# Two loads swapped and the first pieces of a step put in another order, in a one-core encoder trunk

## The reference, cut to what matters

```python
D_MODEL = 1024; SEQ = 256; N_MEM = 256
D_FF = ((8 * D_MODEL // 3 + 127) // 128) * 128      # 2816

def rms_norm(x, g):
    xf = x.astype(jnp.float32)
    y = xf * lax.rsqrt(jnp.mean(xf * xf, axis=-1, keepdims=True) + EPS)
    return (y * g.astype(jnp.float32)).astype(x.dtype)

def swiglu_half_step(h, norm_g, w_gate_up, w_down):
    hn = rms_norm(h, norm_g)
    gate, up = jnp.split(hn @ w_gate_up, 2, axis=-1)
    return h + 0.5 * ((jax.nn.silu(gate) * up) @ w_down)

# in every layer i, h = x at first:
h = swiglu_half_step(h, ffn1_norm[i], ffn1_w_gate_up[i], ffn1_w_down[i])
z = rms_norm(h, mix_norm[i]) @ w_in[i]
# memory attention: kv = rms_norm(mem, mem_norm_g) @ w_mem_kv, then softmax(q k) v
h = h + jnp.concatenate([y_mix, y_mem], axis=-1) @ w_out[i]
h = swiglu_half_step(h, ffn2_norm[i], ffn2_w_gate_up[i], ffn2_w_down[i])
```

## Time and profile before

| | before |
|---|---|
| median of three runs | 964.34 us |
| profiled execution, its own time | 966.0 us |
| profiled execution, span from first to last instruction | 964.2 us |
| TensorE busy | 946.4 us, 98% |
| VectorE busy | 557.1 us, 58% |
| ScalarE busy | 462.8 us, 48% |
| mean granted clock of TensorE | 0.991 |
| moved by DMA | 167.06 MB, mean 173 GB/s |

### The profile page before, as it was taken

How to read it: one execution, slowest core, us unless ns; L and a number is a source line. 1 busy time by engine, 2 the same in 40 slices (tenths; PEclk the granted TensorE clock), 3 DMA queues, 4 the chain that set the end, 5 groups by cost and what they waited for, 6 DMA issues and landing times.

```text
span 964.2 us, 13364 instructions
## 1 busy us (share of the span) xinstructions
PE 946.4 (98%) x4482; PEld 778.9 (81%) x4482; DVE 557.1 (58%) x680; ACT 462.8 (48%) x644; POOL 40.9 (4%) x71
## 2 busy tenths in 40 slices
PE   8899999999999999999999999999989999999998
PEld 5788888887888888888878888888867888888887
DVE  5555464584566655454777455556665666455553
ACT  5554453564446444444555354454564365354451
POOL 1000100100000000000100000000120000000000
PEclk9999999999999999999999999999997999999999
DMA  9766756555037746565276656565520256656551
GB/s 300 227 197 208 235 178 216 163 158 176 30 110 232 217 153 207 172 195 197 88 222 215 217 156 205 162 209 183 174 88 1 88 179 217 215 158 207 160 172 44
DMA packets 136704, 167.06 MB, mean 173 GB/s; under 512 B 10600, under 2 KB 101456, under 8 KB 136672
## 3 DMA queue, kind: packets, MB, share of 16 engines
q1 hardware_dynamic: 135472, 164.67, 54.4%
q0 software_dynamic: 1024, 1.90, 0.8%
q10 hardware_dynamic: 176, 0.07, 0.0%
HBM read 165.55 MB, written 1.05 MB: 173 GB/s over the span
## 4 chain that ended last, share of the span: by engine, by line
PE 94%; DVE 2%; ACT 2%; DMA 1%; issue 1%; POOL 0%; SPq 0%; DVEq 0%; ACTq 0%; POOLq 0%
PE ps L1350 21%; PE ps L1352 21%; PE ps L1351 21%; PE ps L1419 8%; PE ps L1421 8%; PE ps L1423 8%; PE ps L1403 2%; PE ps L1285 1%; DMA w_raw<-in_ffn_w_gate_up_dram 1%; PE ps L1518 1%; PE ps L1554 1%; PE ps L1539 1%; PE ps L1602 1%; PE ps L1559 0%; DVE w_lo L876 0%
## 5 line engine op out<-in xcount | busy, mean ns | idle before, releaser
L876 DVE TENSOR_TENSOR w_lo<-w_raw,w_hi 128x1024 fp32r<-128x1024 f32 x296 | 356.9, 1223 | 157.3 <-ACT w_hi L579 154.6
L579 ACT CAST w_hi<-w_raw 128x1024 fp32r<-128x1024 f32 x296 | 304.9, 1049 | 145.6 <-PE ps L1423 71.9
L1350 PE MATMUL ps<-w_hi,mainT_hi 128*128 128x512 f32 x768 | 305.5, 398 | 4.1 <-DVE w_lo L876 2.4
L1352 PE MATMUL ps<-w_hi,mainT_lo 128*128 128x512 f32 x768 | 300.2, 391 | 0.0
L1351 PE MATMUL ps<-w_lo,mainT_hi 128*128 128x512 f32 x768 | 299.8, 390 | 0.0
L1350 PEld LDWEIGHTS ps<-w_hi,mainT_hi 128*128 128x128 f32 x768 | 144.5, 188 | 36.2 <-DVE w_lo L876 4.7
L1352 PEld LDWEIGHTS ps<-w_hi,mainT_lo 128*128 128x128 f32 x768 | 144.6, 188 | 31.0
L1351 PEld LDWEIGHTS ps<-w_lo,mainT_hi 128*128 128x128 f32 x768 | 144.8, 189 | 28.5
L632 ACT ACTIVATE silu_g<-ps,row_rs 128x256 f32<-128x256 f32 x88 | 41.8, 475 | 228.6 <-PE ps L1352 228.6
L961 DVE SCALAR_TENSOR_TENSOR act_f<-ps,row_rs,silu_g 128x256 f32<-128x256 f32 x88 | 42.6, 484 | 163.3 <-ACT silu_g L632 163.3
L1419 PE MATMUL ps<-w_hi,actT_hi 128*128 128x512 f32 x320 | 99.1, 391 | 0.0
(11 more groups left out here) (185 smaller groups left out, 666.3 us busy)
## 6 DMA issues: line engine op xcount, KB each, us to landing
w_raw<-in_ffn_w_gate_up_dram SPq DMA_DIRECT2D x352, 256.0 KB, 3.6
w_raw<-in_ffn_w_down_dram SPq DMA_DIRECT2D x176, 256.0 KB, 4.2
w_raw<-in_w_in_dram SPq DMA_DIRECT2D x32, 256.0 KB, 3.4
w_raw<-in_w_out_dram SPq DMA_DIRECT2D x32, 256.0 KB, 3.6
w_raw<-in_w_mem_kv_dram SPq DMA_DIRECT2D x16, 256.0 KB, 3.6
w_raw<-in_w_kv_dram SPq DMA_DIRECT2D x8, 256.0 KB, 3.3
ycat<-in_mem_dram SPq DMA_DIRECT2D x1, 1024.0 KB, 7.3
out_dram<-h SPq DMA_DIRECT2D x4, 256.0 KB, 2.0
```

Of the source, the lines that this page charges most:

```text
L579: ins = nc.scalar.copy(half(w_hi[s], b), half(w_raw[s], b))
L876: ins = nc.vector.tensor_tensor(half(w_lo[s], b), half(w_raw[s], b), half(w_hi[s], b).bitcast(F32), ALU.subtract)
L1350: pe.matmul(dst, x_hi, wh, start=start, stop=False)
L1352: return pe.matmul(dst, x_lo, wh, start=False, stop=stop)
```

## The change

Four pieces of code are reordered; no instruction is added, removed or altered.

1. SyncE: the second gate unit of step 1 is issued before the memory's DMA; it was behind it.
2. TensorE: the turns of part 1 of both tiles stand ahead of piece (0, 1); they were behind it.
3. VectorE: `low_first(1)` stands ahead of `scale_first(1)`, and `split_gained(1)` ahead of `split_first(1)`.
4. ScalarE: `split_gained(1)` stands ahead of `split_first(1)`.

```diff
@@ sync
                     if name == "ffn0":
+                        load_gate_up(name, 1, (1,))
                         sp.dma_start(ycat[:, :, :], a["mem"][0].rearrange("(t p) d -> p t d", p=P)).then_inc(mem_landed, 16)
-                        load_gate_up(name, 1, (1,))
@@ scalar
             split_gained(0)
             high_first(1)
+            split_gained(1)
             split_first(1)
-            split_gained(1)
             high_first(2)
@@ vector
             split_gained(0)
+            low_first(1)
             scale_first(1)
-            low_first(1)
+            split_gained(1)
             split_first(1)
-            split_gained(1)
             low_first(2)
@@ tensor
                 first_piece(0, 0)
-                first_piece(0, 1)
                 turn_first(0, 1)
                 turn_first(1, 1)
+                first_piece(0, 1)
                 first_piece(1, 0)
```

## The result

| | before | changed |
|---|---|---|
| median of the 18 runs compared | 964.43 us (959.85 to 972.4) | 959.73 us (955.59 to 962.13) |
| ratio, 95% interval | | 0.9937 (0.991 to 0.9964) |
| profiled execution, own time and span | 966.0, 964.2 | 957.53, 955.7 |
| mean granted clock | 0.991 | 0.998 |

Its interval is wide, 3.5 to 8.7 us, and holds the 4.4; these runs do not tell 4.4 from 6.1. The profiled executions, one of each kernel, differ by 8.5 us. The next rows say what of this belongs to the place of the change.

A forecast was written before the change was run, and what follows sets the result against it. TensorE, busy 98% of the span, was taken as the bound, leaving only idle and lower-clock time to win. Earlier matmul 2.70 us plus full clock 1.67 gave 4.4, so 964.34 - 4.4 = 959.9 us, range 958.8 to 961.8.

The forecast's parts named there:

- What bounds it: TensorE busy 98% of 964.2 us; at step 1's second gate/up unit, waiting costs 2.58 us and half clock 1.67.
- The memory's turn: SyncE's queue: the memory ahead delays the second gate/up unit 2.6 us; moved last, the unit's first half lands at 21.8.
- Landing to matmul: Second gate/up unit of step 1: cast, subtraction and hand-overs take 2.36 us from landing to first matmul.
- The first pieces: Start of TensorE's work: reordering brings later pieces about 1.0 us earlier, hidden by the unit's landing; 0.15 us credited.
- The sum: Second unit's first matmul at 24.05 instead of 26.75 saves 2.70 us; full clock over 12 matmuls saves 1.67; together 4.4.
- the shift goes through to the end: Behind the second unit's product TensorE works without a gap, so the whole 4.4 us reaches the end: 959.9 us.
- no stretch at half clock before 700 us: Sign of being right: TensorE's clock does not fall to half anywhere before 700 us.
- The bounds: Limits at the second unit: gain 3.7 us if it lands later, 5.3 if sooner, 2.7 if half clock stays.
- (a): Rival, chance 0.07: at the activations' turns the memory lands late, near 28.7; TensorE waits 1.5 us, time 961.4.
- (b): Rival, chance 0.03: the memory lands behind 29.6, the clock falls again; slower, up to 966.7 us.
- (c): Rival, chance 0.07: clock still falls before or within the second unit's product, as TensorE stands 1.0 us; 961.6.
- (d): Rival, chance 0.05: the unit's landing is set by its own issue and load contention; 0 to 1 us won, 963.8.

The follow-up runs named there:

- memory alone: Against the kernel before, only the memory's DMA was moved behind the second gate unit of step 1: 960.97 us, ratio 0.995.
- the pieces alone: Against the kernel before, only the TensorE, VectorE and ScalarE reorderings, with the memory's DMA still ahead of the second gate unit: 963.53 us, ratio 0.9979.
- the second set's profile: Profile from a repeat of the changed kernel without further edit; that set's median was 957.55 us, ratio 0.9939, and the profiled execution's span 964.6 us.
- before, filled twice: Kernel before plus repeated head turns in layer 1's attention wait and twelve identity transposes in layer 0's: 959.78 us.

## Why the prediction was right in its mechanism and wrong in its range

- **What bounds it: right for the place of the change.** The 2.58 + 1.67 us of the start were what was won there.
- **The memory's turn: right.** Unit cast at 21.65 (memory alone) and 22.0 (change) against a landing of 21.8 forecast, memory landed at 26.2 against 25.9, and half of it ahead cost about half. Over all eight profiled executions with the memory behind it, the unit is cast at 21.6 to 22.8.
- **Landing to matmul: right.** 24.38 - 22.01 = 2.37 against 2.36 us.
- **The first pieces: right that they are hidden; no run shows the 0.15 us credited** for earlier issues. The piece behind the turn of x began at 11.11 against 11.15 forecast, and TensorE was at the unit 1.1 us earlier (forecast 1.0). But the down weights were issued 0.9 us sooner and landed at 20.5, not 20.15.
- **The sum: a little high.** 4.4 was 2.70 + 1.67; the trace has 2.37 + 1.34. In the first, the 0.15 is missing and the unit landed 0.2 later. In the second I let the product run without a hole: the unit's second half held it until 25.99, and behind each of the two waits the next matmul starts 0.33 to 0.34 us later instead of 0.23. Measured over many runs with the attention filled it is 3.8. That the start of before had just this wait and this half clock was one draw: its wait was 2.4 to 3.6 us in three profiles, and the start's worth is 2.5, 4.0 or 5.9 us by the clock.
- **The step that failed: "the shift goes through to the end", so that 964.34 - 4.4 is the time.** I took the median of three runs, 964.17 to 964.61, for the kernel's one time and 1.7 us as the difference to the profiled one. It was one rung of a ladder from 959.9 to 972.6, and three runs had all fallen on it by chance. The sum also says that TensorE works "without a gap" behind the start. It does not: it waits 2.84 us in layer 1's attention, with a clock of 0.54 behind it in 722 to 737. I knew of this stretch (the signs speak of "no stretch at half clock before 700 us") and took it for a constant, because the diff does not touch it. Its instructions are the same in both kernels, but each execution draws its length anew: none with the pieces alone, 3.4 us and over 16 us in two profiles of the changed kernel. In them the shift was 3.71 us at 718 us and 8.47 us behind the stretch. The bounds had no term for it. The 4.4 us lie within both intervals (3.5 to 8.7 for the first sets, 4.2 to 6.7 for all), so what they do not cover is the spread between sets. That the median of 959.73 came so near 959.9 was luck for the same reason.
- **The rivals:** a late memory (a), with a clock that fell in the wait for it (b), came only where I provoked it, and by another way. (c) and (d) did not occur in the five profiled executions with the changed start, where the clock stayed 1.00 and the unit was cast at 21.6 to 22.3. One sign did fail: in the second set's profile there was a stretch at half clock before 700 us, at 253.

## What to carry to other kernels

A large transfer that is wanted late cost every one behind it in the same queue its full turn (2.6 us for 1 MB here); move it behind those that are wanted first. But look whether the queue can run dry while loads stand behind a wait for a slot. Before promising a few microseconds, look for waits of TensorE of 1.5 to 3 us anywhere in the kernel: here they made the time a ladder, and three runs sat on one rung. Filling such a wait with harmless repeats on TensorE (identical values, the signal on the last) took the ladder away from the changed kernel and made a change of 0.4% visible in 9 and 12 runs.

## What the runs showed of the hardware

- Whether the clock falls behind a given wait, and for how long, differs between executions of the same program. Around waits of 2.2 to 3.9 us at the start it fell in all five profiled executions that have one (before 2.42; 3.91, 3.61, 3.05 and 2.23 in the experiments), for 3.4 us in three of them and 6.8 us in two; behind waits of 0.6 to 1.7 us there it did not. Yet behind the 1.5 us in layer 0's attention it fell in the profiled execution shown above, and behind the 2.8 us in layer 1's it did not in that of the reordered pieces alone (first head turn at 723.40; the stretch behind it, granted clock 1.00):

```profile
723.40:730.00 6.60, 6.60 (x58) 5.41 (x60) 4.26 (x12) 5.16 (x22) 0.00 (x0) 1.00 0.01 2
```

- In before, filled twice, 4 of 12 runs are at a clock of 1.000 and 958.4 us: there the start's wait cost no clock either. Unfilled, none of 112 runs of before was below 959.85. If the start (no loss in 5 of 24 filled runs) and the attentions (none in 5 of 42 runs of the change) were drawn independently, about 3 would be expected. None is few, but not enough to say that they are not.
- Earlier issue into a queue that is already full moved no landing: the down weights were issued 0.9 us sooner and landed 0.4 later. With the memory ahead, the unit was issued at 16.17, 15.76, 15.35 and 15.07 us in four executions, and cast at 24.39, 24.64, 24.79 and 24.76.
